# Up projections by quads: two block products of each pair of tiles split once more

## What is computed

```python
def conv_ffn(x, w_up, conv_w, conv_b, w_down):
    h = x @ w_up                       # 512x1024 by 1024x5632
    c = h.shape[-1]
    h = lax.conv_general_dilated(h, conv_w[:, None, :], window_strides=(1,),
        padding=[(CONV_WIDTH - 1, 0)], feature_group_count=c, ...) + conv_b   # width 3, along tokens
    a, u = jnp.split(h, 2, axis=-1)
    return (jax.nn.gelu(a, approximate=True) * u) @ w_down
```

## Time and profile before

| | us |
|---|---|
| median of 3 runs | 2158.77 |
| lowest, highest | 2157.18, 2158.89 |
| the profiled execution | 2158.03 |
| its span, first to last instruction | 2156.1 |
| PE busy in it | 2127.5 |
| DVE busy | 1183.2 |
| ACT busy | 756.2 |
| GpSimd busy | 5.3 |

### The profile page before, as it was taken

One profiled execution on the slowest core, in us unless ns is written; L12 is line 12 of the kernel. 1 busy time (PEld: TensorE's weight loads), 2 busy tenths in 40 slices (PEclk: granted clock), 3 DMA queues, 4 the chain that ended last, 5 costly groups with the idle time before them and its releaser, 6 DMA issues.

```text
span 2156.1 us, 37799 instructions
## 1 busy us (share of the span) xinstructions
PE 2127.5 (99%) x14808; PEld 1511.7 (70%) x14808; DVE 1183.2 (55%) x2724; ACT 756.2 (35%) x1719; POOL 5.3 (0%) x13
## 2 busy tenths in 40 slices
PE   7999999999999999999999999999999999999998
PEld 3555555558688888865486888888868556585557
DVE  7555555535766652354347666631758667443554
ACT  2444444433223320145432332200322454224553
POOL 0000000000000000000000000000000000000000
PEclk9999999999999999999999999999999999999999
DMA  3111111031222231211112222322341111221112
GB/s 119 64 35 35 35 35 36 31 124 57 87 78 97 78 127 54 93 40 40 59 59 98 78 97 78 105 105 81 84 100 69 50 40 59 78 79 39 34 46 78
DMA packets 25952, 149.96 MB, mean 70 GB/s; under 512 B 2928, under 2 KB 3824, under 8 KB 13264
## 3 DMA queue, kind: packets, MB, share of 16 engines
q1 hardware_dynamic: 24768, 144.28, 19.0%
q0 software_dynamic: 1040, 3.64, 1.3%
HBM read 145.32 MB, written 2.59 MB: 69 GB/s over the span
## 4 chain that ended last, share of the span: by engine, by line
PE 97%; DVE 2%; ACT 0%; issue 0%; DMA 0%; SPq 0%; DVEq 0%
PE banks L2109 20%; PE banks L1503 12%; PE banks L2823 9%; PE banks L2602 5%; PE banks L1422 4%; PE banks L2451 4%; PE banks L529 3%; PE banks L506 3%; PE banks L539 3%; PE banks L2079 3%; PE banks L1346 2%; PE banks L642 2%; PE banks L2485 2%; PE banks L1305 2%; PE banks L2463 2%; PE banks L3562 2%
## 5 line engine op out<-in xcount | busy, mean ns | idle before, releaser
L2109 PE MATMUL banks<-arena 128*128 128x256 f32 x2016 | 436.4, 379 | 0.0
L2109 PEld LDWEIGHTS banks<-arena 128*128 128x128 f32 x2016 | 381.8, 189 | 55.1 <-issue 1.0
L1503 PE MATMUL banks<-arena 128*128 128x256 f32 x1232 | 267.5, 378 | 0.0
L1503 PEld LDWEIGHTS banks<-arena 128*128 128x128 f32 x1232 | 232.3, 189 | 33.5
L2823 PE MATMUL banks<-arena 128*128 128x256 f32 x880 | 194.1, 380 | 0.0
L2823 PEld LDWEIGHTS banks<-arena 128*128 128x128 f32 x880 | 165.6, 189 | 30.2 <-issue 5.1
L2164 ACT ACTIVATE arena<-banks 128x256 f32<-128x256 f32 x180 | 69.3, 385 | 298.1 <-PE banks L2109 298.1
L2324 DVE SCALAR_TENSOR_TENSOR arena<-arena 128x511 f32<-128x511 f32 (+1 forms) x144 | 108.2, 751 | 74.6 <-ACT arena L2173 57.5
L2521 ACT ACTIVATE arena<-arena 128x128 f32<-128x128 f32 (+3 forms) x192 | 101.5, 530 | 100.0 <-DVE arena L2553 99.8
L2602 PE MATMUL banks<-arena 128*128 128x512 f32 x256 | 124.6, 614 | 0.0
L2553 DVE CUSTOM_DVE_ANT_0 arena<-banks,arena 128x256 f32<-128x256 f32 (+3 forms) x160 | 70.8, 472 | 72.5 <-PE banks L2451 72.4
(11 more groups left out here) (362 smaller groups left out, 3255.8 us busy)
## 6 DMA issues: line engine op xcount, KB each, us to landing
arena<-up SPq DMA_DIRECT2D x44, 1024.0 KB, 4.7
arena<-down SPq DMA_DIRECT2D x16, 1408.0 KB, 6.1
arena<-w_mix SPq DMA_DIRECT2D x18, 512.0 KB, 3.5
arena<-o_in SPq DMA_DIRECT2D x8, 1024.0 KB, 4.9
arena<-q SPq DMA_DIRECT2D x8, 512.0 KB, 3.4
arena<-o_attn SPq DMA_DIRECT2D x4, 1024.0 KB, 4.6
arena<-e_gate SPq DMA_DIRECT2D x4, 1024.0 KB, 4.9
arena<-e_o SPq DMA_DIRECT2D x4, 1024.0 KB, 4.9
```

Of the source, the lines that this page charges most:

```text
L1503: ins = pe.matmul(ps[:, bank, LO], w[:, t, :], x[:, t, :], start=first and t == 0, stop=t == last, skip_group_check=not first)
L2109: ins = pe.matmul(out, w[:, q, :], x[:, q, :], start=start and q == 0, stop=q == 3, skip_group_check=not start)
```

## The change

Two tiles (tile 0 in slot 0, tile 1 in slot 1) are now taken together as a quad; a layer has 9 quads (`QUADS`), one to a pass of the loop. P1, P3, P5, P6, P7 of each tile stay as they are. P2 of both tiles (weights a12 of tile 0 and of tile 1, same tokens) becomes one product of 2x2 blocks called `a`, P4 of both tiles (a22, same tokens T4) one called `b`: the two tiles are its two output blocks, its input channels are halved (2 tiles each), its tokens too (128 each). Each is done with seven inner products of two fp32 matmuls on 128 tokens (aP1 to aP7, bP1 to bP7), where there were 16 matmuls of 256 tokens in P2 and P4 of two tiles before. The inner weight sums (aS1 to bS4, 256 elements per partition each) are made on GpSimd, the inner token sums on DVE once a layer, the copies of 128 columns on ACT. The inner sums stand in PSUM banks 0 to 3. Since P2 and P4 no longer go into the tile's own PSUM, the joins are other ones: e (u2 of a or b to a copy), c11 and c21 from PSUM for tile 0, and for tile 1 w (two copies of 128) and c11, c21 in two halves of 128.

```diff
-        for s in range(2):
-            self.seven_tensor(pe, layer, 0, s, True)
-        with pe.Fori(1, SEVENS // 2) as i:
-            for s in range(2):
-                self.seven_tensor(pe, layer, i, s)
+        self.quad_tensor(pe, layer, 0, True)
+        with pe.Fori(1, QUADS) as i:
+            self.quad_tensor(pe, layer, i)
...
+    def quad_tensor(self, pe, layer, i, first=False):
...
+        def inner(name, g, x, d, w, tokens, start):
+            for q in range(2):
+                ins = pe.matmul(ps[:, inner_bank[g][x], d * P:d * P + P], w[:, q, :], tokens[:, q, :], start=start and q == 0,
+                                stop=q == 1, skip_group_check=not start)
+                if name == "bP7" and q == 0:
+                    k.begun(ins, 1)
+            S.done(ins, name)
...
+        outer("P1_0", 0, 0, a11, h[:, 0::2, LO], True)
...
+        outer("P5_0", 0, 1, self.s["S1"], self.t[0], True)
...
+        outer("P6_0", 0, 0, self.s["S2"], self.t[1], False)
...
+        outer("P3_0", 0, 1, self.s["S4"], h[:, 1::2, HI], False)
...
+        outer("P7_0", 0, 0, self.s["S3"], self.t[2], False)
...
+        outer("P1_1", 1, 0, self.raw(1)[0], h[:, 0::2, LO], True)
+        pe.wait_ge(J.sem, J.at(layer, i, "c12_1", -1))
+        pe.wait_ge(W.sem, W.at(layer, i, 1, "S1"))
+        outer("P5_1", 1, 1, self.s["S1"], self.t[0], True)
+
+        pe.wait_ge(J.sem, J.at(layer, i, "c21_1l", -1))
         turned(4)
-        product("P4", y, a22, self.t[3], False)
+        for g in "ab":
+            inner(g + "P1", g, 0, 0, self.inner_raw(g, 0, 0), self.inner_tokens(g, 0, 0), True)
+        for g in "ab":
+            inner(g + "P2", g, 1, 0, self.inner_raw(g, 0, 1), self.inner_tokens(g, 1, 0), True)
+        for j, g in enumerate("ab"):
+            pe.wait_ge(G.sem, G.at(layer, i, g + "S1"))
...
+            inner(g + "P5", g, 1, 1, self.inner_s[g + "S1"], self.inner_t[g][0], False)
+        for j, g in enumerate("ab"):
+            pe.wait_ge(G.sem, G.at(layer, i, g + "S2"))
...
+            pe.wait_ge(A.sem, A.at(layer, i, g + "p1"))
+            inner(g + "P6", g, 0, 0, self.inner_s[g + "S2"], self.inner_t[g][1], False)
...
+            pe.wait_ge(A.sem, A.at(layer, i, g + "p5"))
+            inner(g + "P3", g, 1, 1, self.inner_s[g + "S4"], self.inner_tokens(g, 1, 1), False)
...
+            pe.wait_ge(A.sem, A.at(layer, i, g + "u2"))
+            inner(g + "P7", g, 0, 0, self.inner_s[g + "S3"], self.inner_t[g][2], False)
...
+        outer("P6_1", 1, 0, self.s["S2"], self.t[1], False)
...
+            pe.wait_ge(A.sem, A.at(layer, i, g + "u3"))
+            inner(g + "P4", g, 0, 0, self.inner_raw(g, 1, 1), self.inner_t[g][3], False)
...
+        outer("P3_1", 1, 1, self.s["S4"], h[:, 1::2, HI], False)
...
+        outer("P7_1", 1, 0, self.s["S3"], self.t[2], False)
...
+    def quad_scalar(self, act, layer, i, conv, first=False):
+
+        self.part_scalar(act, layer, i, "p1_0")
         if not first:
...
+            self.ident_scalar(act, layer, i, -1, 0, conv)
+        self.part_scalar(act, layer, i, "p5_0")
         if not first:
...
+            self.ident_scalar(act, layer, i, -1, 1, conv)
+        self.part_scalar(act, layer, i, "u2_0")
         if not first:
...
+            self.gelu_scalar(act, layer, i, -1, conv)
+        for name in ("u3_0", "p1_1", "p5_1"):
+            self.part_scalar(act, layer, i, name)
+        for name in ("ap1", "bp1", "ap5", "bp5", "au2", "bu2", "au3", "bu3"):
+            self.inner_scalar(act, layer, i, name)
+        for m in range(2):
+            self.ident_scalar(act, layer, i, 0, m, conv)
+        self.part_scalar(act, layer, i, "u2_1")
+        self.gelu_scalar(act, layer, i, 0, conv)
+        self.part_scalar(act, layer, i, "u3_1")
...
+    def inner_pool(self, pool, layer, i, first=False):
+
+        k, S, G = self.k, self.products, self.inner_weights
+        for s in range(2):
+            pool.wait_ge(k.landed[s], i * 16 + (TURN[f"up{layer}"] + PLAIN // 2 + 1) * 16)
+        if not first:
+            pool.wait_ge(S.sem, S.at(layer, i, "bP7", -1))
+        for name in ("S1", "S2", "S4", "S3"):
+            for g in "ab":
...
+                G.done(pool.tensor_tensor(self.inner_s[g + name], x, y, op), g + name)
...
+    def quad_vector(self, dve, layer, i, conv, last=False):
...
+        self.weight_vector(dve, layer, i, 1, "S1")
+        self.weight_vector(dve, layer, i, 1, "S2")
+        dve.wait_ge(A.sem, A.at(layer, i, "u3_0"))
+        J.done(dve.tensor_tensor(row[0][:, HI], ps[:, UP + 1, LO], p["u2_0"], ALU.add), "c12_0")
+        J.done(dve.tensor_tensor(row[1][:, HI], p["u3_0"], p["p5_0"], ALU.add), "c22_0")
+        self.weight_vector(dve, layer, i, 1, "S4")
+        self.weight_vector(dve, layer, i, 1, "S3")
+        for g, name in (("a", "p1_0"), ("b", "u3_0")):
+            dve.wait_ge(A.sem, A.at(layer, i, g + "u2"))
+            J.done(dve.tensor_tensor(p[name], inner[g][:, 0:2 * P], p[name], ALU.add), "e" + g)
...
+            J.done(dve.tensor_tensor(row[m][:, LO], ps[:, 2 * m + 1, LO], p[name], ALU.add), ("c11_0", "c21_0")[m])
         for m in range(2):
...
+            self.conv_vector(dve, layer, i, 0, m, conv)
+        self.gated_vector(dve, layer, i, 0, conv)
+        for g in "ab":
+            dve.wait_ge(A.sem, A.at(layer, i, g + "u3"))
...
+        if not last:
+            self.weight_vector(dve, layer, i, 2, "S1")
+
+    def quad_end_vector(self, dve, layer, i, conv, last=False):
...
+        if not last:
+            self.weight_vector(dve, layer, i, 2, "S2")
...
+        J.done(dve.tensor_tensor(row[0][:, HI], ps[:, UP + 3, LO], p["u2_1"], ALU.add), "c12_1")
+        lower("a", 0, "p1_1")
+        if not last:
+            self.weight_vector(dve, layer, i, 2, "S4")
...
+        J.done(dve.tensor_tensor(row[1][:, HI], p["u3_1"], p["p5_1"], ALU.add), "c22_1")
+        lower("b", 1, "u3_1")
+        self.conv_vector(dve, layer, i, 1, 0, conv)
+        if not last:
+            self.weight_vector(dve, layer, i, 2, "S3")
+        self.conv_vector(dve, layer, i, 1, 1, conv)
+        self.gated_vector(dve, layer, i, 1, conv)
+        self.cross_vector(dve, layer, i + PLAIN // 2)
```

More of the change, by code:

```diff
@@ L2100, in raw, with inner_raw @@
         return [ring[:, m, odd::2, :] for m in range(2) for odd in range(2)]
[L2102 to L2107, removed]
-            for q in range(4):
-                ins = pe.matmul(out, w[:, q, :], x[:, q, :], start=start and q == 0, stop=q == 3, skip_group_check=not start)
-                if name == "P1" and q == 0:
-                    k.begun(ins, s)
+    def inner_raw(self, g, r, c):
+        return self.raw(r)[{"a": 1, "b": 3}[g]][:, 2 * c:2 * c + 2, :]
@@ L2120, in seven_tensor @@
+        landed(0)
+        pe.wait_ge(A.sem, A.at(layer, i, "u3_0", -1))
         if first:
[L2121 to L2124, removed]
+            pe.wait_ge(self.taps, 8 + 4 * (layer * FT + 1))
+        outer("P1_0", 0, 0, a11, h[:, 0::2, LO], True)
+        pe.wait_ge(J.sem, J.at(layer, i, "c12_0", -1))
@@ new lines, in quad_tensor @@
+        pe.wait_ge(A.sem, A.at(layer, i, "p5_0"))
+        pe.wait_ge(W.sem, W.at(layer, i, 0, "S4"))
+        outer("P3_0", 0, 1, self.s["S4"], h[:, 1::2, HI], False)
+        pe.wait_ge(A.sem, A.at(layer, i, "u2_0"))
+        pe.wait_ge(W.sem, W.at(layer, i, 0, "S3"))
+        turned(3)
+        outer("P7_0", 0, 0, self.s["S3"], self.t[2], False)
+        landed(1)
+        pe.wait_ge(A.sem, A.at(layer, i, "u3_1", -1))
+        if first:
+            pe.wait_ge(self.taps, 8 + 4 * (layer * FT + PLAIN))
@@ new lines, in inner_scalar @@
+    def inner_scalar(self, act, layer, i, name):
+        A, S, J = self.parts, self.products, self.joined
+        g = name[0]
+        product, bank, d, place, until = {"p1": ("P1", 0, 0, 0, "c11_0"), "u2": ("P6", 0, 0, 1, "c11_0"), "u3": ("P7", 0, 0, 2, "c11_1"),
+                                          "p5": ("P5", 1, 1, 3, "wa")}[name[1:]]
+        act.wait_ge(S.sem, S.at(layer, i, g + product))
+        if g == "b":
+            until = {"c11_0": "c21_0", "c11_1": "c21_1", "wa": "wb"}[until]
+        act.wait_ge(J.sem, J.at(layer, i, until, -1))
+        A.done(act.activation(self.inner_part[g][:, place * P:place * P + P],
+                              self.k.ps[:, {"a": 0, "b": 2}[g] + bank, d * P:d * P + P], ACT.Copy), name)
@@ L2172, in ident_scalar @@
+    def ident_scalar(self, act, layer, i, s, m, conv):
+        J = self.joined
+        row = s % 2
+        name = (("c11_0", "c21_0"), ("c11_1", "c21_1"))[row][m]
+        act.wait_ge(J.sem, J.at(layer, i, name, -1 if row else 0))
+        if m == 0:
+            act.wait_ge(self.used, i * 2 + (2 + layer * FT + PLAIN + s))
         col = i * 8 + (layer * 2 * FT * 4 + m * FT * 4 + 4 * (PLAIN + s))
-        act.activation(conv[m], self.row[m], ACT.Identity, scale=self.k.vec("conv", col + 2),
+        act.activation(conv[m], self.row[row][m], ACT.Identity, scale=self.k.vec("conv", col + 2),
```

(14 more changed lines are left out.)

235 lines of the change are left out of this document (141 added, 94 removed).

## The result

The changed kernel takes 2241.3 us (median of 4 runs, 2239.1 to 2244.4) against 2158.3 (median of 4), a ratio of 1.0386 with a 95% interval of 1.0368 to 1.0404. The profiled execution took 2239.7 us, its span 2237.9: 81.7 us more than the profiled one of before. The forecast was 2230 with a range of 2172 to 2266.

What follows compares the result with a forecast made beforehand. PE, busy 99%, was taken to bound the kernel before. From 2158 us: -12.2 (PE), +31.5 (16 passes standing at P5_1), +0.4 (tails), +48 (GpSimd delaying DVE), +4 (first passes) gave 2230 us, range 2172 to 2266.

Steps and rivals of the forecast that it cites:

- the stand: PE idle in front of P5_1, waiting for DVE's S1_1: about 1.95 us a pass without GpSimd's effect.
- the holding up: GpSimd's sums delay DVE's taps, gate, cross sums and S1_1: 3.0 us a pass, +48 us over 16 passes.
- PE's own sum: PE's matmul records per pass: 23.55 us instead of 24.23, -12.2 us over 18 passes.
- ring: Loop of waits from P5_1 through PE, ACT and DVE to the next P5_1: 25.5 us a pass, +31.5 us.
- the first passes: First pass of each layer: 1.1 us of spare, then 2 us lost to GpSimd's sums each, +4 us.
- The upper bound of 0.1275: Most a 128-column PE record might cost, in us, from a line's busy mean; PE's pass then 24.44 us.
- the gap that was set against it: DVE's existing gap of some 0.12 us, subtracted from each GpSimd sum of 0.55 us.
- faster: Rival: PE never waits at P5_1, DVE's run from first tap to S1_1 under 14.9 us; 2146 us, 5%.
- The tails: Layer ends, before the down projection: PE waits 0.1 to 0.3 us a layer for DVE, +0.4 us.
- the ring alone: Rival: DVE's order makes PE stand at P5_1, GpSimd's sums cost DVE nothing; 2178 us, 26%.
- the long sums: Rival: GpSimd's sums take 0.82 to 1.0 us and delay DVE; 2270 to 2295 us, 7%.
- inner products that don't gain: Rival: PE's 128-column records take 0.1275 us; 12 to 14 us more on any case, no separate chance given.

Runs made afterwards that it cites:

- both edits: Changed kernel with S1_1 of the next pass moved ahead of gate and cross sums, and GpSimd's sums cut to one column except in first passes: 2146.8 us.
- one-column sums: Changed kernel with GpSimd's sums cut to one column each in all passes but the first of a layer: 2176.8 us.
- filled: Changed kernel with 8 extra matmuls of 256 columns (16 records) behind P1_1, where PE stood idle: 2213.9 us.

## Why the prediction came out

The forecast, its direction and the place of the stand were right; the sum of 72 us for a measured 81.7 hides one term that was too large and one that was missing. That the two nearly made up for each other is luck: with the holding up at its measured 37 us and no clock, the forecast would have been some 2215, not 2230. By the differences of the runs:

| term | forecast us | measured us | by which runs |
|---|---|---|---|
| PE's own sum | -12.2 | -11.9 | both edits against before |
| ring | +31.9 | +30.0 | one-column sums, less both edits |
| holding up, with the first passes | +52 | +37 | filled, less one-column sums |
| clock | 0 | +26 | profiled execution of the change, less filled |
| together | +72 | +81 | |

The first three terms rest on single runs of three of the kernels; the kernel before varied from 2157.2 to 2160.1 in all. The run with one-column sums kept whole sums in the first pass of each layer, so its 30.0 has the 2.6 us of their stands; the 37 has none of them, where the forecast's 52 has 4. The terms start from the median of 2158.75, the 81.7 from the profiled execution of before, 0.7 lower.

PE's own sum. The record of 128 columns was read right from seven of them: 48 in a row took 5.36 us, 0.112 each, here in the chain in order of time (start, us):

```profile
576.56 5.36 PE banks L2158 x48
```

The upper bound of 0.1275 from the group's mean was off, since each short run there carries the tail of its last record.

The ring. It closed at 25.27 us where 25.5 was summed, a stand of 1.60 for 1.95. The step that carried the forecast, that DVE's share says nothing and its order everything, was shown by moving one instruction: same load, 91 us less. The rival "faster" had its point right, a run of DVE of under 14.9 us: that order gets there by leaving gate and cross sums (3.3 us) out of the ring.

The holding up. A sum of 0.55 us was taken; all eight fall in the ring, and the sum's own turn is 0.58. The step that failed is the gap that was set against it, 0.12 us. The timeline shows the turns, two narrow windows of the changed kernel, ends being start plus duration:

```profile
681.71 1.17 POOL L2450 TENSOR_TENSOR arena<-arena 128x256 f32<-128x256 f32 x1
```

```profile
682.45 0.98 DVE L2463 SCALAR_TENSOR_TENSOR arena<-arena 128x510 f32<-128x510 f32 x1
682.85 1.17 POOL L2450 TENSOR_TENSOR arena<-arena 128x256 f32<-128x256 f32 x1
```

A sum ends at 682.88, the tap that waited for it at 683.43, the next sum at 684.02: the engines take turns, 0.55 us for a tap and 0.58 for a sum, and an instruction's record holds its wait too (a tap has 0.75 without GpSimd, 0.98 here). The same holds all along: in 142 of the 144 sums of the changed kernel a sum ends 0.58 to 0.59 us behind the end of a DVE instruction. A tap's turn is 0.55, but without GpSimd the next one starts 0.90 after it; so for some 0.35 us DVE isn't at the operands, and between two taps a sum costs only 0.58 - 0.35 = 0.23. The run with one-column sums shows DVE's gaps at the other instructions, from S3_0 to S1_1, and two of GpSimd's sums, which have two elements each there:

```profile
668.63 0.69 DVE L2433 TENSOR_TENSOR arena<-arena 128x512 f32<-128x512 f32 x1
669.25 1.64 DVE L2466 SCALAR_TENSOR_TENSOR arena<-arena 128x511 f32<-128x511 f32 x2
670.15 0.19 POOL L2453 TENSOR_TENSOR arena<-arena 128x2 f32<-128x2 f32 x1
670.31 0.64 POOL L2453 TENSOR_TENSOR arena<-arena 128x2 f32<-128x2 f32 x1
671.14 0.69 DVE L2472 TENSOR_TENSOR arena<-arena 128x512 f32 x1 [0.26 <-DVE arena L2466]
672.22 0.43 DVE L2413 TENSOR_TENSOR arena<-arena  x1 [0.39 <-DVE arena L2472]
672.57 0.42 DVE L2414 TENSOR_TENSOR arena<-arena  x1
673.13 0.43 DVE L2416 TENSOR_TENSOR arena<-arena  x1
673.75 0.43 DVE L2418 TENSOR_TENSOR arena<-arena  x1 [0.18 <-DVE arena L2416]
674.38 0.69 DVE L2433 TENSOR_TENSOR arena<-arena 128x512 f32<-128x512 f32 x1 [0.21 <-issue]
```

```profile
687.98 1.17 DVE L2433 TENSOR_TENSOR arena<-arena 128x512 f32<-128x512 f32 x1
```

From the end of S3_0 to the end of S1_1 DVE takes 5.75 us here (669.32 to 675.07) and 7.99 in the changed kernel (681.16 to 689.15, the last row). The difference, 2.24, is all of the growth of the stand, from 1.60 to 3.85. Eight sums' turns are 4.7 us, and DVE's own gaps take in 2.4 of them, 0.30 a sum on average where the forecast had 0.12. The gaps differ: the first cross sum loses 0.06 us, as DVE is idle in front of it anyway, the second 0.5, as without GpSimd it follows the first directly. A copy's turn, 0.26, is shorter than the gap between two taps, so the taps beside copies weren't longer at all.

The rule of the Trainium skill that was weighed in the prediction ("SBUF — State Buffer", Who interferes with whom: a DVE instruction with two SBUF inputs contends with a GpSimd instruction that reads SBUF, and not with one that only writes) agrees with the runs: the sums hold DVE's taps up and are held up by them, one after the other and each for its whole turn, the copies do so too with turns of 0.26 us, and memsets aren't noticed at all. What the rule alone doesn't give is the price, as half of each turn vanishes in DVE's own gaps. The estimate of 0.82 us a sum that the prediction worked out from the Trainium skill ("GPSIMD Engine Reference", Elementwise) was too long for the turn of 0.58; records of 0.90 to 1.17 us are sums that waited.

The clock was missing altogether. The forecast took PE's stand at its own length. That it stood in the ring, where what PE loses afterwards is lost for the ring too, made the 26 us.

The first passes stood 1.30 us each, where 2 were taken. The tails and the DMA loads hardly showed: PE's idle time in front of the down projection's matmuls is 0.1 us in all, where 0.4 was summed.

Of the rivals, the ring alone (2178) was built and gave 2176.8; the long sums (0.82 to 1.0 us each) did not show, as a sum's turn is 0.58, nor did inner products that don't gain. PE never waited in front of an inner product.

## What to carry to other kernels

Where engines with fixed lists feed each other in a loop, add up each ring from an instruction back to itself one pass later, waits of one engine in the list of another included: where the longest ring is longer than every engine's own work, it sets the pass, and the share of busy time of an engine (72% here) tells nothing of it. The cure here was an order, not an engine: an instruction that the waiting engine needs goes ahead of those that nobody waits for. Work given to GpSimd beside a DVE with two operands in SBUF is not free when it reads SBUF too: a pass lost 2.25 us to eight sums, 0.46 to eight copies and nothing to eight memsets, and the sums spared DVE hardly more than they cost.

## What the runs showed of the hardware

- A PE that stands may get the lower clock (1.2 GHz) around the time when it goes on. Behind stands of 3.74 to 3.86 us the granted clock fell in 15 of 16 passes (1.93 to 2.08 us: 7 of 14; 1.30 to 1.77 us: none), and that cost some 1.7 us each time, nearly half of the stand again. Matmuls that do nothing, in the place of the stand, brought 26 us.
- DVE's instructions with two operands in SBUF and GpSimd's instructions that read SBUF take strict turns: 0.55 us for 511 elements on DVE and 0.28 for 256; on GpSimd 0.58 for a sum of 256 elements and 0.26 for a copy. Memsets on GpSimd take no turn. A sum of two elements has a record of 0.19 us where it doesn't wait; one that waited for a tap (0.64) ends 0.06 us behind it, so nearly all of a turn is the elements.
- Float32 records of 128 columns follow each other at 0.112 us, of 256 at 0.2163, so half the columns take 52% of the time.
